# Shorter norm chains, first modulations by halves, rotary halves by transfers, in a two-layer hybrid backbone

## The reference, cut to what matters

```python
sh1, sc1, g1, sh2, sc2, g2 = split(silu(cond) @ ada_w + ada_b, 6)     # per channel
h  = rmsnorm(x, norm1_g) * (1 + sc1) + sh1
p  = h @ w_in                       # q, k, v of three attentions, input of the Fourier mixer
# rotary embedding of latent q, k of two attentions (swa: heads of 64, diff: heads of 32):
#   per half head: concat(x1*cos - x2*sin, x2*cos + x1*sin)
br = [neighbourhood attn, windowed attn, Fourier mixer, differential attn]
x  = x + g1 * (sum_b sigmoid(h @ w_gate_b + b_gate_b) * (br_b @ w_branch_b)) @ w_o
h2 = rmsnorm(x, norm2_g) * (1 + sc2) + sh2
x  = x + g2 * (silu(h2 @ w_a) * (h2 @ w_b)) @ w_ffn_out
# at the end y = rmsnorm(x, final_norm_g)
```

## Time and profile before

| | us |
|---|---|
| median of 3 runs | 2361.34 (2360.16 to 2363.97) |
| the profiled execution's own time | 2361.76 |
| its span in the trace | 2360.0 |
| PE busy in the span | 2280.5 |
| DVE, ACT busy | 941.2, 711.2 |

### The profile page before, as it was taken

How to read it: one execution, slowest core, us unless ns; L and a number is a source line. 1 busy time by engine, 2 the same in 40 slices (tenths; PEclk the granted TensorE clock), 3 DMA queues, 4 the chain that set the end, 5 groups by cost and what they waited for, 6 DMA issues and landing times.

```text
span 2360.0 us, 37061 instructions
## 1 busy us (share of the span) xinstructions
PE 2280.5 (97%) x15562; PEld 2157.1 (91%) x15562; DVE 941.2 (40%) x1712; ACT 711.2 (30%) x1059; POOL 0.2 (0%) x4
## 2 busy tenths in 40 slices
PE   5999999999999999999989999999999999999997
PEld 4899898888988999999989988988899899999997
DVE  4124545555444222222341255455654522322234
ACT  4223344334323221122232233433333322212221
POOL 0000000000000000000000000000000000000000
PEclk8999999999999999999999999999999999999998
DMA  6532221111433332222445233111124122212221
GB/s 269 213 133 102 90 81 48 45 46 47 146 111 98 134 112 81 62 78 76 147 161 176 84 96 109 42 45 46 57 73 164 54 80 71 94 58 72 75 80 67
DMA packets 63120, 225.47 MB, mean 96 GB/s; under 512 B 6176, under 2 KB 9760, under 8 KB 62880
## 3 DMA queue, kind: packets, MB, share of 16 engines
q1 hardware_dynamic: 63008, 223.88, 28.1%
HBM read 217.30 MB, written 6.55 MB: 95 GB/s over the span
## 4 chain that ended last, share of the span: by engine, by line
PE 92%; DVE 4%; DMA 2%; ACT 1%; issue 1%; SPq 0%; DVEq 0%; ACTq 0%
PE lp L511 76%; PE ss L661 4%; PE ss L622 2%; PE ss L643 2%; PE ss L569 1%; DMA wst<-wo 1%; PE ss L577 1%; DMA adae<-adb 1%; PE ss L629 1%; PE ss L740 1%; PE ss L770 1%; DVE wr L1136 0%; DVE tmp L1189 0%; DVE st L1229 0%; PE ss L593 0%
## 5 line engine op out<-in xcount | busy, mean ns | idle before, releaser
L511 PE MATMUL lp<-H,wr 128*128 128x320 f32 x9600 | 1487.6, 313 | 22.2 <-DVE H L1145 8.5
L511 PEld LDWEIGHTS lp<-H,wr 128*128 128x128 f32 x9600 | 1422.2, 189 | 44.2 <-issue 35.2
L1136 DVE TENSOR_TENSOR wr<-wst,wr 128x1024 fp32r<-128x1024 f32 (+2 forms) x236 | 318.8, 1351 | 459.3 <-ACT wr L863 458.0
L863 ACT ACTIVATE wr<-wst 128x1024 fp32r<-128x1024 f32 (+2 forms) x236 | 272.5, 1155 | 434.1 <-PE lp L511 421.5
L511 PEld LDWEIGHTS lp<-G,wr 128*128 128x128 f32 x2112 | 309.9, 188 | 0.8 <-issue 0.8
L511 PE MATMUL lp<-G,wr 128*128 128x320 f32 x2112 | 310.6, 310 | 0.0
L511 PE MATMUL lp<-BR,wr 128*128 128x320 f32 x960 | 163.7, 316 | 7.7 <-DVE wr L1136 5.9
L511 PEld LDWEIGHTS lp<-BR,wr 128*128 128x128 f32 x960 | 144.1, 189 | 11.4 <-issue 6.4
L1161 DVE SCALAR_TENSOR_TENSOR x<-lp,mod,x 128x128 f32 (+1 forms) x144 | 54.5, 434 | 226.3 <-PE lp L511 226.3
L661 PEld LDWEIGHTS ss<-V,pts 128*128 128x128 f32 x720 | 90.9, 192 | 17.5 <-ACT pts L920 10.2
L1446 DVE TENSOR_TENSOR tmp<-lp,tmp 128x640 f32<-128x640 f32 x44 | 36.3, 824 | 170.6 <-PE lp L511 170.6
(11 more groups left out here) (132 smaller groups left out, 1142.5 us busy)
## 6 DMA issues: line engine op xcount, KB each, us to landing
wst<-wff SPq DMA_DIRECT2D x88, 512.0 KB, 3.5
wst<-wgu SPq DMA_DIRECT2D x64, 640.0 KB, 4.0
sm<-adb SPq DMA_DIRECT2D x17, 2048.0 KB, 8.5
wst<-win SPq DMA_DIRECT2D x36, 512.0 KB, 3.5
wst<-wfa SPq DMA_DIRECT2D x16, 768.0 KB, 4.3
bt<-bias SPq DMA_DIRECT2D x32, 320.0 KB, 3.3
wst<-wfb SPq DMA_DIRECT2D x16, 640.0 KB, 3.9
adae<-adb SPq DMA_DIRECT2D x4, 2048.0 KB, 20.0
```

Of the source, the lines that this page charges most:

```text
L511: mm = pe.matmul(out[:, h, 0:TH], w[wi], act[:, ai, k, h * TH:(h + 1) * TH], start=first and i == 0, stop=last and i == 2)
L863: act.activation(wr[:, s, 0, 0:w], wst[:, s, 0:w], ACT.Copy).then_inc(w_hi[s], 1)
L1136: ve.tensor_tensor(wr[:, s, 1, 0:w], wst[:, s, 0:w], wr[:, s, 0, 0:w].bitcast(F32), ALU.subtract).then_inc(w_lo[s], 1)
```

## The change

- **Norms.** The last (eighth) square is no longer added by DVE: `norm_sum` does five matmuls on `sqacc` (seven squares) and then five more on the eighth square in `tmp[:, 3]`, into the same columns. The diagonal tiles and the product with ones are replaced by five PE transposes of the broadcast reciprocal (`norm_spread`), which now follow `norm_sum` at once; the second `modulate` moves behind them. Norm1 uses norm2's form (`normed`, `normed_hi`); ACT's copy to `rstd` and the separate gain and shift steps are gone.
- **Start of layer 0.** `adae` is loaded by halves of the channels: pieces 0 and 1 hold shift and scale of channels 0 to 511, pieces 2 and 3 those of 512 to 1023, each piece by two transfers. `con` is loaded in two parts, the second last; `vc` and the first weights come behind the first half. PE does `modulate`, `norm_sum`, `norm_spread`, `modulate`, `turn_group` for half 0; `first_pair` starts on k = 0 to 3; half 1 is done inside it, its two `modulate` behind k = 2 and its `turn_group` behind k = 3 (`behind_tile`).
- **Rotary.** PE's permutation is gone. In the projections SP writes each of the seven tiles to DRAM (`to_memory`, two copies interleaved by blocks of w = 32 or 16 rows, 256 KB each), and in pairs 1 to 7 loads it back shifted by half a block into `tmp[:, 0]`; DVE does `rotated`, three operations, in pairs 2 to 8, with the sign as a scalar that two reductions make once.

```diff
 # SP
-            sy.dma_start(con[:], cst).then_inc(ld_c, 16)
-            sy.dma_start(vc[:], vec[0]).then_inc(ld_v, 16)
+            sy.dma_start(con[:, 0:C_RS], cst[:, 0:C_RS]).then_inc(ld_c, 16)
             sy.dma_start(x[:], xT).then_inc(ld_x, 16)
...
+            def to_memory(l, c):
+                n = [i for i, _ in TURNS].index(c)
+                to = rq[n].rearrange("(b i r) t -> i b r t", i=2, r=TURNS[n][1])
+                for i in range(2):
+                    sy.dma_start(to[i], qk[:, c, NCTX:T]).then_inc(st_r, 16)
...
             for i in range(2 * AG_E):
-                if i == 2 * AG_E - 1:
+                half, q = i // 2, i % 2
+                for part in range(2):
+                    sy.dma_start(adae[:, i, :, 512 * part:512 * part + 512],
+                                 adb[0, KD * part + 4 * q:KD * part + 4 * q + 4].rearrange("c p k -> p c k")
+                                 [:, :, 512 * half:512 * half + 512]).then_inc(ld_a[i], 16)
+                if i == 1:
+                    sy.dma_start(vc[:], vec[0]).then_inc(ld_v, 16)
                     for s in range(2):
                         weight(0, W_IN, win, 0, s)
-                sy.dma_start(adae[:, i], adb[0, 4 * i:4 * i + 4].rearrange("c p k -> p c k")).then_inc(ld_a[i], 16)
+            sy.dma_start(con[:, C_RS:], cst[:, C_RS:]).then_inc(ld_c2, 16)
             for l in range(L):
                 for c in range(2, IN_A + IN_B):
                     weight(l, W_IN, win, c // 2, c % 2)
+                    out = c - 4
+                    if out in (SWA_Q, SWA_Q + 1, DIFF_Q, DIFF_Q + 1, DIFF_K, DIFF_K + 1):
+                        sy.wait_ge(drained[out % 2], 1 + l * PER_DR + out // 2 + 1)
+                        to_memory(l, out)
...
+                to_memory(l, SWA_K)                      # behind the five okT stores
...
+                    n = p + 1 - TURN_AT                   # in the loop over pairs, behind the job weights
+                    if 0 <= n < len(TURNS):
+                        w = TURNS[n][1]
+                        sy.wait_ge(st_r, 32 * len(TURNS) * (l + 1))
+                        if n:
+                            sy.wait_ge(roped, l * len(TURNS) + n)
+                        else:
+                            sy.wait_ge(br_lo, l * PER_BR + 2)
+                        sy.dma_start(tmp[:, 0, 0:NLAT], rq[n].rearrange("(b r) t -> b r t", r=2 * w)[:, w // 2:w // 2 + w, :])\
+                            .then_inc(ld_t, 16)
 # PE
             def norm_sum(n):
-                pe.wait_ge(sqs, n)
+                pe.wait_ge(sqs, n * SQS + SQS)
                 for t in range(TILES):
-                    mm = pe.matmul(ss[0][:, 0, t:t + 1], sqacc[:, t * P:(t + 1) * P], ones[:, 0:1], start=True, stop=True)
+                    pe.matmul(ss[0][:, 0, t:t + 1], sqacc[:, t * P:(t + 1) * P], ones[:, 0:1], start=(t == 0), stop=False)
+                pe.wait_ge(sq, n * SQ + SQ)
+                for t in range(TILES):
+                    mm = pe.matmul(ss[0][:, 0, t:t + 1], tmp[:, 3, t * P:(t + 1) * P], ones[:, 0:1], start=False,
+                                   stop=(t == TILES - 1))
             def norm_spread(n):
+                pe.wait_ge(inverse, n + 1)
                 for t in range(TILES):
-                    pe.wait_ge(diag, n * TILES + t + 1)
-                    mm = pe.matmul(sflat[0][:, t * P:(t + 1) * P], ones, rstd[:, t * P:(t + 1) * P], start=True, stop=True)
+                    mm = pe.transpose(sflat[0][:, t * P:(t + 1) * P], rt[:, t:t + 1].to_broadcast([P, P]), ident)
...
+                    pe.wait_ge(ld_a[0], 32)               # layer 0, ahead of the projections
+                    modulate(lp[0], four(adae[:, 0]), 0)
+                    norm_sum(0)
+                    norm_spread(0)
+                    pe.wait_ge(ld_a[1], 32)
+                    modulate(lp[0], four(adae[:, 1]), 1)
+                    turn_group(1, MODS_EARLY)
...
+                    def second_half():
+                        pe.wait_ge(mods_half, 1)
+                        for q in range(2):
+                            pe.wait_ge(ld_a[2 + q], 32)
+                            modulate(ss[1], four(adae[:, 2 + q]), q)
+                    def turn_second():
+                        turn_group(2, MODS_EARLY + 2 * KD)
                     if c == 0:
-                        first_pair(l, W_IN, S_H1)
+                        first_pair(l, W_IN, S_H1, {} if l else {HK - 2: second_half, HK - 1: turn_second})
...
-                        pe.matmul(ss[0][:, 0, :], con[:, TURNS[n][1]:TURNS[n][1] + P], qk[:, TURNS[n][0], NCTX:T],
-                                  start=True, stop=True).then_inc(rot, 1)
...
 # in norm2, and alike in norm1 of layer 1
                 modulate(ss[1], four(sm), 0)
-                norm_sum(l * 2 * KD + 2 * KD)
+                norm_sum(2 * l + 1)
+                norm_spread(2 * l + 1)
                 quad_in(1, 2)
                 modulate(ss[1], [smc[:, 0, :], smc[:, 1, :], smc[:, 2, :], smc3[:, 0, :]], 1)
-                norm_spread(2 * l + 1)
 # DVE
+            def normed(n, which, shift, k0=0, k1=KD):
+                for k in range(k0, k1 + 2):
+                    if k < k1:
+                        for a, b, c in ((0, NCTX, 0), (NCTX, T, 1)):
+                            m = ve.scalar_tensor_tensor(out=xn[:, k, a:b], in0=x[:, k, a:b], scalar=am[:, which, k, c:c + 1],
+                                                        in1=sflat[0][:, a:b], op0=ALU.mult, op1=ALU.mult)
+                        m.then_inc(norm_x, 1)
+                    if n == 0 and k == 1:
+                        weight_lo((0, W_IN, 0, 1))
+                    if k >= k0 + 2:
+                        ve.wait_ge(h_hi, n * KD + k - 1)
...                                                       # low part of H[:, k - 2], two operations
             def rotated(l, n):
+                ve.wait_ge(ld_t, 16 * (l * len(TURNS) + n + 1))
+                ve.scalar_tensor_tensor(out=tmp[:, 0, 0:NLAT], in0=tmp[:, 0, 0:NLAT], scalar=nsg[:, i:i + 1], in1=rp[i][:, 1, :],
+                                        op0=ALU.mult, op1=ALU.mult).then_inc(rot_read, 1)
+                ve.tensor_tensor(tmp[:, 1, 0:NLAT], qk[:, c, NCTX:T], rp[i][:, 0, :], ALU.mult).then_inc(rot_read, 1)
+                ve.wait_ge(rot_read, 2 * (l * len(TURNS) + n + 1))
+                ve.tensor_tensor(qk[:, c, NCTX:T], tmp[:, 1, 0:NLAT], tmp[:, 0, 0:NLAT], ALU.subtract).then_inc(roped, 1)
...
+            def early_half(half):                         # waits for turn_group; 4 additions, 2 gains, for 4 k tiles
...
+                    weight_lo((0, W_IN, 0, 0))            # layer 0
+                    for half in range(2):
+                        early_half(half)
+                        normed(0, 0, 0, HK * half, HK * half + HK)
 # ACT, layer 0
+                    grow_copy(lp[0], 1)
                     for s in range(2):
                         weight_hi((0, W_IN, 0, s))
-                    grow_copy(lp[1], 2)
+                    act.wait_ge(mods_half, 1)
+                    normed_hi(0, 0, range(HK))
+                    grow_copy(ss[1], 2)
+                    act.wait_ge(mods, 1)
+                    normed_hi(0, 0, range(HK, KD))
```

More of the change, by code:

```diff
@@ L263, in build @@
         h_hi = sem("h_hi")
+        SQ, SQS = KD, KD - 1
         a_f = sem("a_f")
@@ L527, in chunk, with first_pair @@
                 mm.then_inc(lin[s], 1)
-            def first_pair(l, stage, ready):
+            def first_pair(l, stage, ready, behind_tile={}):
                 for s in range(2):
@@ L540, in first_pair @@
                         mm.then_inc(lin[s], 1)
+                    if s and k in behind_tile:
+                        behind_tile[k]()
             def weights(l, stage, j, s):
@@ L867, in jobs_hi, with normed_hi @@
                     weight_hi(behind(l, GATE, n // 2, n % 2))
[L869 to L879 removed]
+            def normed_hi(n, shift, kk=range(KD)):
+                for k in kk:
+                    act.wait_ge(norm_x, n * KD + k + 1)
+                    act.activation(H[:, 0, k, 0:NCTX], xn[:, k, 0:NCTX], ACT.Identity, bias=mod[:, shift + k, 0:1])
+                    act.activation(H[:, 0, k, NCTX:T], xn[:, k, NCTX:T], ACT.Identity, bias=mod[:, shift + k, 1:2])\
+                        .then_inc(h_hi, 1)
             def gate_tanh(l, jobs):
@@ L953, in _ @@
                 act.wait_ge(ld_v, 16 * (l + 1))
+                root(l * 2 + 1)
                 if l == 0:
                     grow_copy(lp[0], 1)
-                act.wait_ge(sqs, l * 2 * KD + KD)
-                root(l * 2 + 1)
-                act.wait_ge(nbc, l * 2 + 1)
-                act.activation(rstd[:], sflat[0][:, 0:T], ACT.Copy).then_inc(nrs, 1)
-                if l == 0:
                     for s in range(2):
                         weight_hi((0, W_IN, 0, s))
-                    grow_copy(lp[1], 2)
-                act.wait_ge(mods, l * 2 + 1)
-                if l:
```

(48 more changed lines are left out.)

156 lines of the change are left out of this document (52 added, 104 removed).

## The result

The changed kernel takes **2366.06 us** (median, 2361.24 to 2368.93) beside 2362.40 for the one before: ratio 1.0017, interval 1.0010 to 1.0024. By the bound of 0.2% that the prediction uses this is no change, by its interval slightly slower; 2339 was forecast. The profiled execution has a span of 2366.7 us, 6.7 more than before, though PE's busy time is hardly changed.

The account below looks back on a forecast made before the run. PE was taken as the bound, busy 2280.5 of 2360.0 us; rotary -11.2, stores and loads 0, norms -12.7 and start +0.9 made -23.0 from 2361.76, 2338.8, given as 2339 after median adjustment and rounding, range 2333 to 2357.

Parts of the forecast that it names:

- The stores and loads of the turns, taken at 0: Projections and pairs: the turns' DRAM transfers make nothing late; 0 us.
- The even spread: Lower end for the turns' transfers: they spread over the engines like the trace's large ones; 0 us.
- rival (a): Turns' stores run on few engines and PE waits for the third `sm` piece: 2351, chance 0.40.
- The upper end: First three turns' stores on 4 of 16 engines: 8.4 us wait plus 3.4 clock in both layers, 11.8.
- The start, +0.9: Layer 0's start by halves: leaves the first pair at 64.3 us against 63.35 before, +0.9.
- the first product at 34.7: Layer 0's start: PE begins its first projection at 34.7 us, 11.8 earlier than before.
- +2.5: Layer 0's start, if the root's table load or slow turns come on top.
- The rotary, -11.2: Pairs: taking the permutation off PE saves 0.8 us in each of 14 turns, -11.2.
- (b): Rival: pairs don't shorten, ACT's copies or DVE's operations set their pace: 2346; chance with (d) 0.12.
- (c): Rival: the load back is late, DVE waits and holds up PE's scores: 2366 or more, chance 0.05.
- The norms, -12.7: Four norms behind layer 0's start: shorter chains save 4.1, 3.2, 2.6 and 2.8 us, together -12.7.
- (d): Rival: broadcast-column transposes cost as much as the old product, 3 us less gain: 2342; chance with (b) 0.12.

Follow-up runs that it names:

- e1: Changed kernel with each turn's two stores writing 128 consecutive rows each, halves not exchanged in memory: 2341.42 us, ratio 0.9913.
- e4: Changed kernel with six stores moved behind the weights of the projection's last six chunks, the seventh behind the pairs' first weights: 2345.19 us, ratio 0.9924.
- e6: Changed kernel with each store of the first three turns issued as four, one per block of 32 rows: 2345.68 us, ratio 0.9930.
- e5: Changed kernel with layer 0's start by whole modulations and four 2 MB loads, as in the kernel before: 2362.80 us, ratio 1.0003.
- e2: Changed kernel with the rotary back on PE, without the turns' stores and loads back: 2356.43 us, ratio 0.9971.
- e10: Kernel before with only the shortened norms; rotary on PE and layer 0's start as before: 2354.65 us, ratio 0.9966.
- e12: Norms-only kernel with W_O's third-tile weights issued ahead of the modulation weights sent when the gates end: 2339.86 us, ratio 0.9907.
- e11: Kernel before with W_O's third-tile weights issued ahead of the modulation weights sent when the gates end: 2351.62 us, ratio 0.9954.

## Why the prediction was wrong

The forecast failed by 27 us, and one step carries nearly all of it.

- **The stores and loads of the turns, taken at 0: wrong.** The even spread was chosen as "the row that is nearest"; e1 against the changed kernel puts the term at +24.7, all of it the stores', rival (a) and more. The rival's mechanism was right: the window with only a load of 4 blocks in flight (237.50 to 238.00) shows a share of 0.25. The Trainium skill, page "DMA: Bandwidth & Descriptors", section "Why a DMA increments its semaphore by 16 and not by 1", has the count: 4 for these shapes, by the slowest dimensions; trace and e1 agree. By its further statement that from SP it is always the lowest-numbered engines, stores that follow each other would add up on the same four; no run here shows which engines they are, but the windows ahead of 237.50 have narrow and wide transfers in one and the same quarter. Rival (a)'s size was short too. At the modulations it had 4.2 of wait and 1.7 of clock; 5.83 and 1.7 came (15 in all with layer 1). And it saw no second place: the seventh turn's stores stand ahead of the pairs' first weights, 7.0 for both layers against the kernel before, 10.0 against e1.
- **Where the choice went astray.** The trace before held no DRAM side of few blocks, so its full engines said nothing for this shape; they counted as a witness against (a) all the same. The upper end then priced one waiting piece and not every transfer queued behind each store.
- **The start, +0.9: mis-sized.** +7.6 came in the trace. The step that failed is the first product at 34.7; it was 42.06. Behind the first modulation the chain was costed at or near the full clock: passes 2.5 (4.5), second modulation 1.92 (3.64), turn 2.34 (3.58), transposes 0.7 (1.33), and 1.28 of table load, which with slow turns the prediction had named at +2.5 but left out of the sum. About 2 us of this are the one execution: in e1, e4 and e6, with the same start, the passes took 2.5 to 2.7 and the first product came at 39.8 to 40.0. From there on the forecast held: 29.6 us from the first product to the pair's end, 28.8 measured, with the hole where it was put. The medians charge 2.8 (after against e5) and 1.3 (e2 against e10, each to its before).
- **The rotary, -11.2: right.** 12.0 in the pairs, (b) and (c) didn't come: no wait of DVE for the load back.
- **The norms, -12.7: right, 11.8** (e12 against e11; 14.6 at the four places in e10's trace, and norm2 of layer 1 adds up to 2.8, not 2.6, by its own terms). (d) didn't come: five transposes took 0.76 at the full clock. The change alone nets 7.3, since W_O's late weights take the rest; that wait, 2.3 to 3.8 us in each of the kernels that keep the old order, wasn't in the forecast.

As a chain of runs, each to its before: norms -7.3 (e10), start +1.3 (e2), rotary -15.0 (e1), stores +24.7 (the changed kernel): +3.7. Of the rotary's 15.0 the pairs show 12.0; W_O's wait is 1.3 and 1.2 us shorter in e1 (2.26 and 2.38) than in e2 (3.58 in both layers), 2.5 of the other 3. Why it comes in these two sizes stays open.

## What to carry to other kernels

Price a transfer by the outermost count of its DRAM side, here 4 blocks against 128 rows, before its bytes; if it is small, ask of every transfer issued after it when it is needed, and split it by blocks or move it to where nothing waits behind it. A witness counts only if it has the same shape: a trace in which all transfers are wide says nothing of a narrow one. Before a shortened stage is booked as gain, look whether the next stage's load is issued by what you shorten or by an older event; here one load behind 4 MB was worth 10.8 us by itself.

## What the runs showed of the hardware

- SyncE itself is held by a narrow transfer's backlog: the same load of 2 MB took 4.14 us to issue behind four stores on few engines, 0.44 behind four wide ones.
- Behind a wait of 2.3 to 2.4 us at one and the same place, 12 products took 2.02 and 2.03 (changed kernel, before) to 3.51 us (e1); the price of a short wait is not that wait alone, and it isn't the same in each kernel.
